# The feed-forward's second product in three rounded products: ScalarE makes the weights' high parts, GpSimd the low parts

## The reference

```python
h = rmsnorm(x, norm_ffn_g[l])
u = causal_dwconv(jnp.einsum("bsd,df->bsf", h, w_up[l]), conv_ffn_w[l])
gate_f, up_f = u[..., :D_FF], u[..., D_FF:]
x = x + jnp.einsum("bsf,fd->bsd", jax.nn.silu(gate_f) * up_f, w_down[l])
```

## Time and profile before

| what | value |
|---|---|
| median of 3 runs | 3966.53 us (3965.98 to 3973.01) |
| the profiled execution's own time | 3973.19 us |
| its span | 3971.4 us |
| PE busy | 3838.2 us (97%) |
| DVE busy | 2845.7 us (72%) |
| ACT busy | 1585.9 us (40%) |
| POOL busy | 88.2 us (2%) |
| mean granted TensorE clock | 0.978 |

### The profile page before, as it was taken

One profiled execution on the slowest core, in us unless ns is written; L12 is line 12 of the kernel. 1 busy time (PEld: TensorE's weight loads), 2 busy tenths in 40 slices (PEclk: granted clock), 3 DMA queues, 4 the chain that ended last, 5 costly groups with the idle time before them and its releaser, 6 DMA issues.

```text
span 3971.4 us, 61257 instructions
## 1 busy us (share of the span) xinstructions
PE 3838.2 (97%) x21282; PEld 3185.6 (80%) x21282; DVE 2845.7 (72%) x5169; ACT 1585.9 (40%) x2439; POOL 88.2 (2%) x101
## 2 busy tenths in 40 slices
PE   8999999899989999999999999999979999999998
PEld 7897789545887888888888888888748888888887
DVE  6442266895788789999887777777463997777776
ACT  5201053231219444444484444444321094444443
POOL 0000000000000000000000000000400000000000
PEclk9899999999999999999999999999979999999999
DMA  5214455475433666666625656666764516666664
GB/s 193 80 45 131 154 182 159 139 239 184 144 113 127 191 197 195 191 190 192 193 77 176 189 188 188 189 190 191 176 237 158 167 58 194 188 188 190 189 187 152
DMA packets 203773, 666.53 MB, mean 168 GB/s; under 512 B 35920, under 2 KB 46176, under 8 KB 202480
## 3 DMA queue, kind: packets, MB, share of 16 engines
q1 hardware_dynamic: 166816, 602.71, 48.2%
q0 software_dynamic: 12496, 52.53, 4.3%
q10 hardware_dynamic: 24320, 9.37, 0.9%
HBM read 637.34 MB, written 26.15 MB: 167 GB/s over the span
## 4 chain that ended last, share of the span: by engine, by line
PE 88%; DVE 9%; ACT 1%; DMA 1%; issue 1%; DVEq 0%; SPq 0%; ACTq 0%; POOLq 0%
PE psum L1083 27%; PE psum L1069 17%; PE psum L1071 9%; PE psum L641 7%; PE psum L720 4%; PE psum L695 4%; PE psum L1160 4%; PE psum L1251 3%; PE psum L1149 2%; DVE arena L2351 1%; PE psum L1049 1%; DVE arena L2352 1%; PE psum L1128 1%; DVE arena L2353 1%; PE psum L1425 1%; PE psum L750 1%
## 5 line engine op out<-in xcount | busy, mean ns | idle before, releaser
L1083 PE MATMUL psum<-rows_split_odd,coef_split 128*128 128x512 f32 x2400 | 590.6, 396 | 3.6 <-DVE rows_split_odd L2495 3.6
L1083 PE MATMUL psum<-rows_split,coef_split 128*128 128x512 f32 x2208 | 532.1, 390 | 0.3 <-issue 0.3
L2500 DVE TENSOR_REDUCE work<-psum 128x256 f32<-128x512 f32 x360 | 249.1, 692 | 394.1 <-PE psum L1071 393.0
L1083 PEld LDWEIGHTS psum<-rows_split_odd,coef_split 128*128 128x128 f32 x2400 | 437.8, 188 | 105.0 <-issue 6.8
L1069 PE MATMUL psum<-input_split,rows_split 128*128 128x512 f32 x1440 | 513.9, 397 | 1.2 <-DVE rows_split L2495 1.2
L1069 PE MATMUL psum<-input_split,rows_split_odd 128*128 128x512 f32 x1440 | 510.0, 393 | 0.0
L1710 ACT ACTIVATE work<-work 128x256 f32<-128x256 f32 x360 | 151.1, 420 | 875.8 <-DVE work L2500 875.8
L2495 DVE TENSOR_TENSOR rows_split_odd<-ring,rows_split_odd 128x1024 fp32r<-128x1024 f32 x380 | 462.6, 1218 | 8.9 <-ACT rows_split_odd L1512 8.9
L1083 PEld LDWEIGHTS psum<-rows_split,coef_split 128*128 128x128 f32 x2208 | 402.0, 188 | 81.4 <-issue 0.9
L1512 ACT ACTIVATE rows_split_odd<-ring 128x1024 fp32r<-128x1024 f32 x380 | 401.3, 1057 | 155.8 <-PE psum L1083 155.4
L2495 DVE TENSOR_TENSOR rows_split<-ring,rows_split 128x1024 fp32r<-128x1024 f32 x364 | 443.0, 1217 | 5.4 <-ACT rows_split L1512 5.4
(11 more groups left out here) (446 smaller groups left out, 5295.0 us busy)
## 6 DMA issues: line engine op xcount, KB each, us to landing
ring<-in_u SPq DMA_DIRECT2D x384, 512.0 KB, 3.6
ring<-in_v SPq DMA_DIRECT2D x384, 512.0 KB, 3.5
ring<-in_w SPq DMA_DIRECT2D x372, 512.0 KB, 3.6
scratch_inj<-stage ACTq DMA_DIRECT2D x16, 512.0 KB, 5.3
arena<-scratch_inj POOLq DMA_DIRECT2D x7, 1024.0 KB, 7.7
scratch_cm<-work POOLq DMA_DIRECT2D x8, 512.0 KB, 5.4
scratch_cm<-arena POOLq DMA_DIRECT2D x8, 512.0 KB, 5.2
arena<-scratch_parked POOLq DMA_DIRECT2D x4, 1024.0 KB, 7.8
```

Of the source, the lines that this page charges most:

```text
L1083: last = mm(bank(2 + 2 * i + f), CFR[:, b, c, P * i:P * i + P], parts[:, v, 512 * f:512 * f + 512], start=(first and c == 0 and v == 0), s ...
L2500: dve.tensor_reduce(AC[:, b, :], bank(b).rearrange("p (x t) -> p t x", x=2), AX, ALU.add)\
```

## The change

The down projection (`split_linear`, in place of `linear`) now takes three products a block, as the up projection does. ScalarE writes the inner activations' high parts (`inner_high`) and VectorE their low parts (`inner_low`), both during the second half of the up projection. The 22 weight slots get their high parts from ScalarE (`weight_high`, into three buffers that take turns, `DH`), and their low parts from GpSimd, which subtracts the high part from the ring slot and writes the result over the slot (`RL` is the ring under another type). PE waits for the low part of each slot. ScalarE's copies stand in its program between its other work: slots 0 to 2 after the last `inner_high`, slots 3 and 4 before it takes `ssm_angle`, and then, ahead of the squares of output tile t (t from 1), those that `down_high(range(...))` gives: 5 to 7, 8 to 10, 11 and 12, 13 to 15, 16 to 18 and 19 to 21 for t = 1 to 6. The copy of slot n (from the fourth on) waits until PE has begun slot n-2.

```diff
 PARKED = (48, 64, 80)
 AHEAD = (0, 10, 14)
 LATE, LATE_WORK = 20, 1150
+DOWN_SEEN = QT_ - PLAIN + 1 + FT - PLAIN + 1
 STEADY = [sum(NEXP - n for n in AHEAD[:p]) for p in range(4)]
 TWO_PI = 6.283185307179586
 C1, C2 = 6.28125, 0.0019350051879882812
...
             return sems[name]
         sb = lambda name, shape, dt=F32: ctx.enter_context(nc.sbuf_tensor(name, shape, dt))
+        with nc.sbuf_tensor("ring_low", [P, RING, SLOT], F32R) as t:
+            RL = t[:, :, :]
         ring = sb("ring", [P, RING, SLOT])
...
+        with nc.sbuf_tensor("inner_split", [P, 2, FK, S], F32R) as t:
+            INNER = (t[:, 0], t[:, 1])
         arena = sb("arena", [P, 32768])
         with nc.sbuf_tensor("coef_split", [P, 2, 2, S], F32R) as t:
             CFR = t[:, :, :, :]
+        with nc.sbuf_tensor("down_high", [P, KD_, P], F32R) as t:
+            DH = [HR[:, :, 0, 0:P], HR[:, :, 0, P:S], t[:, :, :]]
         stage = sb("stage", [P, 1024])
         small = sb("small", [P, NCOLS])
         with nc.sbuf_tensor("rows_split_odd", [P, 2, 2, SLOT], F32R) as t:
...
             shape = list(a.shape)
             shape[at] = n
             return a.to_broadcast(shape)
+
+        def blocks(a, w):
+
+            return a[:, w % RING, :].rearrange("p (k m) -> p k m", k=KD_)
         def halves(a, b, m):
...
         UF = A(0, FT, S)
         SQX = A(12288, 8, S)
-        SQF, SQU, SQN = A(5632, 8, S), A(7680, 8, S), A(9728, 8, S)
+        SQF, SQU, SQN = A(11264, 4, S), view(work, 0, 8, S), A(9728, 8, S)
         Z = A(0, 16, 512)
         ZR = A(8192, 4, 8, P + 1)
         UNUSED = [A(D * n, 8, P) for n in range(1, 4)] + [A(12544, 8, P)]
...
             pool.dma_start(RAWC, io["ssm_c"]).then_inc(sem("tables_loaded"), 16)
             pool.dma_start(LAM, io["ssm_lam"]).then_inc(sem("tables_loaded"), 16)
             pool.dma_start(MIXB.rearrange("p h t -> p (h t)"), io["bs"]).then_inc(sem("tables_loaded"), 16)
+            for i in range(FK):
+                pool.wait_ge(sem("parts_high"), DOWN_SEEN + i + 1)
+                w = SEGS["down"][0] + i
+                pool.tensor_tensor(blocks(RL, w), blocks(ring, w), DH[i % 3].bitcast(F32), ALU.subtract)\
+                    .then_inc(sem("parts_low"), 1)
             for b in range(NPREP):
                 pool.wait_ge(sem("cm_ready"), b + 1)
                 pool.dma_start(io["cm"][GB4 * b:GB4 * b + GB4].rearrange("g p n -> p g n"),
...
                     last = mm(bank(b)[:, 0:n], ones, src[:, k, 0:n], start=(k == 0), stop=(k == kt - 1))
                 L.mark(last, "rowsum")
-            def sum_part(src, k, b=7, per=1):
+            def sum_part(src, k, b=7, per=1, rows=8):
                 if k % per == 0:
                     L.take("squares")
-                last = mm(bank(b)[:, 0:S], ones, src[:, k, 0:S], start=(k == 0), stop=(k == 7))
+                last = mm(bank(b)[:, 0:S], ones, src[:, k % rows, 0:S], start=(k == 0), stop=(k == 7))
                 if k == 7:
                     L.mark(last, "rowsum")
...
             linear(8, 8, MG, S, between=lambda t: sum_part(SQX, t - 1) if t else None)
             sum_part(SQX, 7)
             parted(FT, QT_ - PLAIN + 1)
-            L.take("ffn_inner")
+            def split_linear(tiles, kt, right, high, seen, ready, between=None):
+
+                w0, l0 = L.slots, L.lin
+                evacuated()
+                for t in range(tiles):
+                    if t >= 2:
+                        pe.wait_ge(sem("lin_free"), l0 + t - 1)
+                    for k in range(kt):
+                        if t == 0:
+                            ready(k)
+                        n, c = divmod(t * kt + k, 8)
+                        if c == 0:
+                            pe.wait_ge(sem("parts_low"), seen + n + 1)
+                        out, low = bank(t % 2)[:, 0:S], blocks(RL, w0 + n)[:, c, :]
+                        ins = mm(out, high(n)[:, c, :], right[0][:, k, :], start=(k == 0), stop=False)
+                        if c == 0:
+                            ins.then_inc(sem("slot_begun"), 1)
+                        mm(out, high(n)[:, c, :], right[1][:, k, :], start=False, stop=False)
+                        ins = mm(out, low, right[0][:, k, :], start=False, stop=(k == kt - 1))
+                    ins.then_inc(sem("lin_ready"), 1)
+                    if between:
+                        between(t)
+                L.lin += tiles
+                L.slots += tiles * kt // 8
             def down_beside(t):
                 if t == 1:
                     rowsum(SQU, 8, S, b=6)
                 if t:
-                    sum_part(SQF, t - 1)
-
-            linear(8, FK, UF, S, between=down_beside)
-            sum_part(SQF, 7)
+                    sum_part(SQF, t - 1, rows=4)
+
+            split_linear(8, FK, INNER, lambda n: DH[n % 3], DOWN_SEEN, lambda k: L.take("right_low"), between=down_beside)
+            sum_part(SQF, 7, rows=4)
             def turn_injection(b):
...
                     act.wait_ge(sem("lin_ready"), L.lin + t - 2)
                 copy(UPR[:, (t - PLAIN) % 3, 0, :], ring[:, w % RING, :]).then_inc(sem("parts_high"), 1)
+            def weight_high(name, i, n, dst):
+
+                w = SEGS[name][0] + i
+                act.wait_ge(sem(f"slot_loaded{w % RING}"), 16 * (w // RING + 1))
+                if i >= n:
+                    act.wait_ge(sem("slot_begun"), w - n + 2)
+                copy(dst, blocks(ring, w)).then_inc(sem("parts_high"), 1)
+
             def tap(name, taps, dst, t):
                 act.wait_ge(sem("lin_ready"), L.lin + t + 1)
...
             others(16)
             squares_behind(SQX)
             root(R1[:, 0:S], R2[:, 0:S])
+            def inner_high(j):
+
+                L.take("ffn_inner")
+                L.mark(copy(INNER[0][:, j, :], UF[:, FK + j, :]), "right_high")
+
             input_high(2)
             part_high("up", PLAIN)
             for t in range(FT):
...
                 if 1 <= t <= FK:
                     act.wait_ge(sem("lin_free"), L.lin + t)
                     f(UF[:, t - 1, :], UF[:, t - 1, :], ACT.Silu).then_inc(sem("ffn_gate"), 1)
+                if t > FK:
+                    inner_high(t - 1 - FK)
+            inner_high(FK - 1)
             others(FT)
+
+            def down_high(tiles):
+
+                for i in tiles:
+                    weight_high("down", i, 3, DH[i % 3])
+
+            down_high(range(3))
             act.wait_ge(sem("tables_loaded"), 80)
             L.give(f(TP[:, 0, :], LAM[:, 2, :], ACT.Exp), "exp_done")
+            down_high(range(3, 5))
             L.take("ssm_angle")
             L.do(f(TP[:, 6, :], TP[:, 1, :], ACT.Exp))
             L.do(f(TP[:, 7, :], TP[:, 4, :], ACT.Sin))
-            L.give(f(TP[:, 8, :], TP[:, 5, :], ACT.Sin), "ssm_trig")
+            L.give(f(TP[:, 8, :], TP[:, 5, :], ACT.Sin), "exp_done")
             for t in range(8):
+                if t:
+                    down_high(range((FK * t - 1) // 8 + 3, min((FK * t + FK - 1) // 8 + 3, FK)))
                 act.wait_ge(sem("lin_free"), L.lin + t + 1)
                 if t == 0:
                     L.mark(f(SQU, X[:, :, S:2 * S], ACT.Square), "squares")
-                L.mark(f(SQF[:, t, :], X[:, t, 0:S], ACT.Square), "squares")
+                L.mark(f(SQF[:, t % 4, :], X[:, t, 0:S], ACT.Square), "squares")
                 if t == 4:
                     root(R1[:, S:2 * S], R2[:, S:2 * S])
             L.lin += 8
...
             add_x = lambda t, ps, b: tt(X[:, t, 0:S], ps[:, 0:S], X[:, t, 0:S], ALU.add)
             evacuate(8, add_x, 0)
+            def inner_low(j):
+
+                L.take("right_high")
+                L.mark(tt(INNER[1][:, j, :], UF[:, FK + j, :], INNER[0][:, j, :].bitcast(F32), ALU.subtract), "right_low")
+
             norm_input("norm_ffn")
             seen = QT_ - PLAIN + 1
             input_low(seen)
...
                     j = t - FK
                     dve.wait_ge(sem("ffn_gate"), j + 1)
                     dve.wait_ge(sem("lin_free"), L.lin + t + 1)
-                    ins = tt(UF[:, j, :], UF[:, j, :], UF[:, t, :], ALU.mult)
-            L.give(ins, "ffn_inner")
+                    L.mark(tt(UF[:, t, :], UF[:, j, :], UF[:, t, :], ALU.mult), "ffn_inner")
+                    if j:
+                        inner_low(j - 1)
+            inner_low(FK - 1)
             L.lin += FT
+
             def parameters():
                 dve.wait_ge(sem("tables_loaded"), 80)
```

More of the change, by code:

```diff
@@ L1595, in _ @@
             L.do(f(ROWS[:, 3, :], ROWS[:, 3, :], ACT.Ln, bias=1.0))
-            L.give(f(TSUM[0:8, 0:1], col("a_log")[0:8, :], ACT.Exp), "softplus_parts")
+            L.give(f(TSUM[0:8, 0:1], col("a_log")[0:8, :], ACT.Exp), "exp_done")
             L.take("decay_rows")
@@ L2110, in _ @@
             misc(3)
-            L.take("softplus_parts")
+            L.take("exp_done")
             L.do(stt(ROWS[:, 3, :], AB[0:8, :], 0.0, ROWS[:, 3, :], ALU.max, ALU.add))
@@ L2290, in parameters @@
```

(2 more changed lines are left out.)

## The result

The changed kernel took **3994.96 us** (median of 5 runs, 3988.58 to 4003.96) against 3971.38 us (median of 5 runs, 3965.98 to 3973.01) for the kernel before. The ratio is 1.0065, with a 95% interval of 1.0053 to 1.0077: slower by some 26 us (0.0065 x 3971); the medians lie 23.6 us apart. The forecast of 3986.0 us was 19.5 above the 3966.5 us of three runs before; with five runs that median is 3971.38, and 3994.96 lies inside the range of 3970 to 3996 by 1 us, so the total says little about the mechanism. The profiled execution took 4001.43 us, with a span of 3999.6 us.

What follows compares the result with a forecast made beforehand. TensorE was taken to bound the kernel, holding 88% of the chain that ended last. Terms of +7.0 us without turns and +12.5 for turns made +19.5 on 3966.5: 3986.0 us, range 3970 to 3996.

Steps and rivals of the forecast that it cites:

- products: Down projection's 176 blocks at the up projection's three-product price, 0.361 us a block in place of 0.432: -12.5 us.
- inner low parts on VectorE: Up projection: VectorE's cycle becomes 3.08 us, 0.19 more than TensorE's, in 19 tiles, 1.3 us absorbed: +2.3 us.
- start: Start of the down projection: TensorE begins after 6.1 us in place of 2.09, +4.0 us.
- slots 5, 13 and 16, waits: Down projection, TensorE waiting: slot 5 +4.4, slot 16 +5.0; with turns slot 13 +5.0 and slot 16 later by 4.8.
- clock after stalls: Dips of TensorE's clock to 0.50 after stalls, 1.9 us each: +3.8 us for two, +1.9 for another with turns.
- first tile, end of the last: Down projection's first tile and end of the last, added for VectorE and GpSimd taking turns: +0.8 us.
- part on turns: Down projection: VectorE's two-operand instructions and GpSimd's subtractions exclude each other, +12.5 us, chance 0.50; rival no turns, 0.30.
- the subtraction: GpSimd's low part of each weight slot: 2.4 us, middle of two and three passes, bounds 0.97 and 3.2.
- the places of the stalls: TensorE idle at the start and slots 5 and 16, at 13 with turns; ScalarE's copies queue behind `ssm_angle` and the root.

Runs made afterwards that it cites:

- f_products: Changed kernel without ScalarE's weight copies; PE reads the low parts' buffer for both weight parts, GpSimd fills it with zeros once a slot is loaded: 3964.0 us.
- j_copies: Changed kernel with VectorE's twelve 64x512 copies after the sixth tile replaced by fills of the same size: 3991.8 us.
- h_warm: Changed kernel with 64 more matmuls of 128x256 ahead of slot 16, where PE would wait: 3993.0 us.
- k_fill: k_all with GpSimd filling the low parts' buffer with zeros in place of subtracting: 3959.0 us.
- a_slot5: Changed kernel with ScalarE's copy of slot 5 moved ahead of its wait for `ssm_angle`: 3984.6 us.
- d_fill: Changed kernel with GpSimd filling the low parts with zeros in place of subtracting: 3972.6 us.
- v_low: k_all with VectorE taking the low parts of 20 of the 22 slots: 3959.7 us (median of 5), ratio to before 0.9970.
- b_root: Changed kernel with ScalarE's copies of slots 16 and 17 moved ahead of its root: 3991.2 us.
- v_norm: v_low with all 22 low parts on VectorE, slot 4 copied ahead of the sines, six products moved behind the norm: 3963.0 us (median of 12), ratio to before 0.9979.
- k_all: Changed kernel with every copy moved to where ScalarE is free, two `parameters` steps ahead of the tiles: 3984.1 us (median of 10), ratio to before 1.0024.

## Why the prediction was right or wrong

It had the right sign, the right mechanism at four of five stalls, and 19.5 us where the stretch grew by 25.2. Two terms were too small, by 5.3 and 3.3 us, and one too large, by 2.3, so the sum came closer than its terms. By its own terms:

| term | predicted, us | measured, us |
|---|---|---|
| products | -12.5 | -12.2 (f_products) |
| inner low parts on VectorE | +2.3 | 0 (ahead of the stretch) |
| start | +4.0 | +3.9 (6.02 after the tap, against 2.09) |
| slots 5, 13 and 16, waits | 4.4 + 5.0 + 9.8 = 19.2 | 5.91 + 4.28 + 8.23 = 18.4 |
| clock after stalls | +5.7 | +9.0 |
| first tile, end of the last | +0.8 | +6.1 |
| sum | +19.5 | +25.2 |

(The clock: PE busy 81.9 us in the changed kernel, 71.0 in f_products without a dip, so 10.9, less the 1.9 that before had. The end: idle time grew by 28.4 us, less 3.9 and 18.4. The sums of squares in the dips count under the clock.)

**The step that failed** is the last one of the part on turns, "for the first tile and the end of the last I add 0.8". It came from counting VectorE's two-operand instructions only ("such two-operand reads are all that GpSimd does here, just where VectorE's are densest"), which left the twelve copies out. The runs showed 6.1 us in its place. Each of the last three subtractions held one of the copies up for 2.1 us; then the six products follow, and the last residual add stands behind them in VectorE's program. Nor was there room for a delay any more, and this the rows of before already tell: from the sixth residual add to the last product VectorE has 17.6 us of work (718.39 to 735.99), which two tiles covered at 9.93 us each and no longer cover at 8.4. f_products has the same order and no subtraction; there fills make the copies 2.1 us longer, and PE waits 3.69 us for the last squares, where it waited 0.60 before:

```profile
718.66 0.42 DVE L2319 TENSOR_TENSOR X<-psum,X 128x256 f32<-128x256 f32 x1
725.90 0.42 DVE L2319 TENSOR_TENSOR X<-psum,X 128x256 f32<-128x256 f32 x1
```

The last residual add comes 7.2 us after the one ahead of it, by VectorE's products, and not a tile's 8.4. j_copies is the test of the copies: fills in their place, which aren't held up, give 4.8 of the 6.1 us back. The Trainium skill (SBUF — State Buffer, Who interferes with whom) says more than the sentence that the prediction drew on: copies and `tensor_scalar` can enter modes that take both ports, and then contend too. The trace agrees that they contend, with 2.75 us for a copy of 0.62. It doesn't show such a mode in these copies: their 512 columns in 0.62 us are the pace of the two-operand instructions (1,024 in 1.22), while another copy takes 0.63 us for 1,024 columns:

```profile
709.16 0.63 DVE L2393 COPY arena<-arena 128x1024 f32<-128x1024 f32 x1
```

The prediction's estimate from the Trainium skill (GPSIMD Engine Reference, 3.1), some 2.3 us for the subtraction, is borne out by the 2.34 to 2.40 measured.

**The clock** was the other term that was too small. The prediction gave each dip 1.9 us, read from the one dip of the kernel before; h_warm gives 2.6 us for the one after slot 16. Read microsecond by microsecond, the clock stood at 0.50 for 3.4 us of PE's products in the kernel before, and for some 4.6, 6.0, 5.0 and 5.7 us of them behind the stalls at slots 0, 5, 13 and 16 in the changed one; the 16 products for the other squares fell into the dip after slot 5 (5.02 us by the chain of waits, 3.45 before). What decides how long a dip lasts is open.

**The inner low parts** cost nothing: the 960 matmuls took 115.47 us in six of the experiments' traces, as before. VectorE's cycle came to 2.91 us for 2.89 of PE's, where I had worked out 3.08: back-to-back instructions start a little before the row of the one ahead of them ends (the taps 1.13 us after a low part of 1.22). In the profiled execution of the changed kernel they took 117.04, in f_products 116.95 and in k_fill 117.71; that lies ahead of the stretch, and it is the clock, not the low parts. Soon after the start of these products, long before the first inner low part, the granted clock is at 0.50 for three microseconds:

```profile
534.00:537.00 3.00, 3.00 (x16) 3.00 (x15) 1.92 (x3) 0.37 (x2) 0.00 (x0) 0.50 0.64 175
```

f_products has the same from 536 to 539 us and k_fill from 532 to 535, a_slot5 and the kernel before have 1.00 there. PE had idled 1.80 us ahead of these products and 1.81 us in the kernel before: much the same wait was followed by a dip once and not the other time.

**Right as predicted**: the subtraction (2.4 us; 2.34 to 2.40, where nothing holds it), though it was the middle of two and three passes, which no row backed, and so partly luck; the turns, on which the forecast was chosen from two ends, at 3.3 us an instruction and shown by d_fill, k_fill and v_low; the places of the stalls and what holds ScalarE at each, shown by a_slot5 and b_root. What these two corrected is the notion that a stall could be priced by itself: of the 14.1 us of the two stalls 5.8 came back when both causes were removed. Slot 16's stall was 1.6 us shorter than predicted (8.23 against 9.8), because the two subtractions met another block: they held up three of VectorE's small instructions behind the fourth tile (2.25, 2.42 and 2.29 us in place of 0.22), so the fifth residual add started 3.8 us late, and the root ended 12.0 us after the fifth tile (717.45 to 729.48), where 8.3 + 4.8 = 13.1 had been worked out. PE, at the low clock for a part of it, got to slot 16 in 7.35 us in place of 6.9.

## What to carry to other kernels

Before giving GpSimd work because it is idle, add its busy time to VectorE's in the same stretch: where they take turns, the sum, less what isn't held up, is about what the stretch will take (98.5 us worked out, 97.9 measured in the best of the orders tried here with all the subtractions on GpSimd, 87.9 for the kernel before). A subtraction that takes 2.4 us there and 1.22 on VectorE is then cheaper on VectorE, even if VectorE looks like the fuller engine (82.5 and 74.4 us in v_low and v_norm). And set an engine's longest block against the tiles that cover it after the change: a quicker PE leaves it less room. And when removing one stall's cause gives back less than its length, check what is next on the same queue before removing a second one.

## What the runs showed of the hardware

- **A VectorE copy is held up by a GpSimd subtraction.** 64x512, float32, 0.62 us alone (L2408); 2.74 to 2.75 us beside a subtraction, one copy for each. A `TENSOR_SCALAR` of 128x64 took 2.35 us in k_all in place of 0.20:

```profile
658.46 0.19 DVE L2359 TENSOR_SCALAR arena<-arena 128x64 f32<-128x64 f32 x1
658.69 2.35 DVE L2360 TENSOR_SCALAR arena<-arena 128x64 f32<-128x64 f32 x1
661.07 0.19 DVE L2361 TENSOR_SCALAR arena<-arena 128x64 f32<-128x64 f32 x1
```

- **A GpSimd fill holds up copies, but not two-operand instructions.** Beside fills the six instructions of 1,024 columns stay at 1.22 us, and the twelve copies take 9.54 us, against 6.29 + 1.20 = 7.5 with GpSimd silent (v_norm). VectorE's own fills, and its residual adds with an operand in PSUM (0.42 us), were held up in none of these runs, beside subtractions or fills.
- **The waiting engine's instruction shows the wait inside its length.** In both engines' rows a held-up instruction is long (3.3 us on VectorE, 3.28 on GpSimd), with no idle time before it. Busy shares then overstate the work: 69.0 us for 45.9.
